# The feed-forward's output product with its 544 token columns cut as 512 and 32 instead of 272 and 272

## The reference

```python
def swiglu(x, w_in, w_out):
    gate, up = jnp.split(x @ w_in, 2, axis=-1)      # w_in (1024, 2*2816)
    return (jax.nn.silu(gate) * up) @ w_out         # w_out (2816, 1024)

for l in range(DEPTH):                              # DEPTH = 2
    x = layer_norm(DN_ALPHA * x + 0.5 * swiglu(x, ffn1_w_in[l], ffn1_w_out[l]), ...)
    ...                                             # projections, RWKV-7, attention, gated DeltaNet
    x = layer_norm(DN_ALPHA * x + mix, ...)
    x = layer_norm(DN_ALPHA * x + 0.5 * swiglu(x, ffn2_w_in[l], ffn2_w_out[l]), ...)
```

## Time and profile before

| what | value |
|---|---|
| runs | 2839.8, 2860.64 us; median 2850.22 |
| profiled execution, span | 2839.4 us; the faster run is 0.4 us longer |
| PE matmul busy | 2612.6 us (92%) |
| PE weight loads busy | 2457.6 us (87%) |
| VectorE (DVE) busy | 1667.0 us (59%) |
| ScalarE (ACT) busy | 946.3 us (33%) |
| POOL busy | 161.5 us (6%) |
| DMA | 201.67 MB, mean 71 GB/s |
| mean granted TensorE clock | 0.941 of full speed |

### The profile page before, as it was taken

How to read it: one execution, slowest core, us unless ns; L and a number is a source line. 1 busy time by engine, 2 the same in 40 slices (tenths; PEclk the granted TensorE clock), 3 DMA queues, 4 the chain that set the end, 5 groups by cost and what they waited for, 6 DMA issues and landing times.

```text
span 2839.4 us, 59246 instructions
## 1 busy us (share of the span) xinstructions
PE 2612.6 (92%) x23238; PEld 2457.6 (87%) x23238; DVE 1667.0 (59%) x2503; ACT 946.3 (33%) x1694; POOL 161.5 (6%) x168
## 2 busy tenths in 40 slices
PE   8999999978877899999999999998787789999996
PEld 8999999866665899999999999987666568999996
DVE  5666436665666466663366653477556655666534
ACT  4333224342222243332233332333322324333323
POOL 1030110000000010001100001100000001000011
PEclk9999999987887999999999999999877889999997
DMA  4853324310000323323222323341000022232221
GB/s 109 98 96 89 90 81 124 94 33 5 10 10 22 98 75 89 87 81 90 84 77 87 89 83 89 112 118 46 29 2 9 10 73 69 82 89 84 85 87 57
DMA packets 380501, 201.67 MB, mean 71 GB/s; under 512 B 41461, under 2 KB 376821, under 8 KB 379528
## 3 DMA queue, kind: packets, MB, share of 16 engines
q1 hardware_dynamic: 377928, 197.46, 24.1%
q0 software_dynamic: 2400, 1.82, 2.0%
HBM read 188.07 MB, written 13.34 MB: 71 GB/s over the span
## 4 chain that ended last, share of the span: by engine, by line
PE 76%; DVE 11%; issue 6%; ACT 5%; DMA 1%; SPq 1%; DVEq 0%; POOLq 0%; ACTq 0%; POOL 0%
PE ps L683 54%; PE ps L738 20%; DVE ar L1932 3%; DVE ar L1926 2%; ACT ar L1427 2%; ACT wh L1358 1%; DVE wl L1810 1%; SPq L530 1%; PE ps L1014 1%; DVE x L1926 1%; DMA raws<-in_ffn_w_in 0%; DVE ar L1962 0%; DVE xl L1917 0%; DVE ar L1929 0%; DMA raws<-in_w_in 0%
## 5 line engine op out<-in xcount | busy, mean ns | idle before, releaser
L1810 DVE TENSOR_TENSOR wl<-raws,wh 128x1024 fp32r<-128x1024 f32 x336 | 411.3, 1225 | 662.1 <-ACT wh L1358 658.0
L683 PE MATMUL ps<-xh,wh 128*128 128x272 f32 x2880 | 604.8, 291 | 17.7 <-DVE wl L1810 15.2
L683 PE MATMUL ps<-xh,wl 128*128 128x272 f32 x2880 | 599.7, 290 | 0.0
L683 PE MATMUL ps<-xl,wh 128*128 128x272 f32 x2880 | 598.2, 289 | 0.0
L738 PE MATMUL ps<-ar 64*64 64x64 f32 (+12 forms) x5408 | 423.5, 270 | 140.0 <-ACT ar L1427 37.1
L738 PEld LDWEIGHTS ps<-ar 64*64 64x64 f32 (+5 forms) x5408 | 317.2, 157 | 224.5 <-issue 58.8
L1358 ACT ACTIVATE wh<-raws 128x1024 fp32r<-128x1024 f32 x336 | 354.9, 1057 | 408.3 <-PE ps L683 375.9
L683 PEld LDWEIGHTS ps<-xh,wh 128*128 128x128 f32 x2880 | 457.5, 190 | 21.6 <-DVE wl L1810 17.9
L683 PEld LDWEIGHTS ps<-xl,wh 128*128 128x128 f32 x2880 | 457.7, 190 | 0.0
L683 PEld LDWEIGHTS ps<-xh,wl 128*128 128x128 f32 x2880 | 457.2, 190 | 0.0
L683 PE MATMUL ps<-hh,wh 128*128 128x272 f32 x1408 | 292.2, 289 | 0.0
(11 more groups left out here) (190 smaller groups left out, 2678.4 us busy)
## 6 DMA issues: line engine op xcount, KB each, us to landing
raws<-in_ffn_w_in SPq DMA_DIRECT2D x176, 512.0 KB, 3.6
raws<-in_ffn_w_out SPq DMA_DIRECT2D x64, 512.0 KB, 4.0
raws<-in_w_in SPq DMA_DIRECT2D x42, 512.0 KB, 3.7
raws<-in_ffn_w_out SPq DMA_DIRECT2D x32, 384.0 KB, 3.4
raws<-in_w_out SPq DMA_DIRECT2D x16, 448.0 KB, 3.9
x_kept<-x SPq DMA_DIRECT2D x2, 2176.0 KB, 10.2
x<-x_kept SPq DMA_DIRECT2D x2, 2176.0 KB, 8.0
ar<-in_consts SPq DMA_DIRECT2D x2, 1337.5 KB, 6.7
```

The costliest lines, as they stand in the source:

```text
L683: ins = pe.matmul(ps[:, bank + h, 0:n1 - h * NH], w[u % 2][:, k, :], a[:, k0 + k, h * NH:n1], start=(first and k == 0 and n == 0), stop=(l ...
L1810: dve.tensor_tensor(wl[u % 2][:, :, :], raw[u % 2][:, :, :], wh[u % 2][:, :, :].bitcast(F32), ALU.subtract).then_inc(sem("wl_done"), 1)
```

## The change

The matmul helper cuts the columns at 512 (`SEQ`) instead of at 272 (`NH`) where the activations are `hh`, that is in the output product alone. The first matmul of each pair fills one bank with 512 columns, the second puts the last 32 into the next bank. The residual reads the 544 results as one contiguous run over both banks (`tokens`) instead of as two runs of 272 (`bank2`). Everything else stays.

```diff
+        def tokens(b):
+            return ps[:, b:b + 2, :].rearrange("p a n -> p (a n)")[:, 0:NT]
...
                     for n, (w, a) in enumerate(((wh, hi), (wh, lo), (wl, hi))):
+                        cut = SEQ if hi is hh else NH
                         for h in range(2):
-                            n1 = a.shape[2] if h else NH
-                            ins = pe.matmul(ps[:, bank + h, 0:n1 - h * NH], w[u % 2][:, k, :], a[:, k0 + k, h * NH:n1],
+                            n1 = a.shape[2] if h else cut
+                            ins = pe.matmul(ps[:, bank + h, 0:n1 - h * cut], w[u % 2][:, k, :], a[:, k0 + k, h * cut:n1],
                                             start=(first and k == 0 and n == 0), stop=(last and k == nblocks - 1 and n == 2))
...
-                dve.scalar_tensor_tensor(out=halves(chunk(x, c + u)), in0=halves(chunk(x, c + u)), scalar=ALPHA, in1=bank2(2 * u),
+                dve.scalar_tensor_tensor(out=chunk(x, c + u), in0=chunk(x, c + u), scalar=ALPHA, in1=tokens(2 * u),
                                          op0=ALU.mult, op1=ALU.add).then_inc(sem("z_done"), 1)
```

## The result

The changed kernel takes 3039.27 us in the median of two runs (3034.34 and 3044.19), against 2850.22 before: a ratio of 1.067, 95% interval 1.063 to 1.071. The profiled execution took 3044.19 us with a span of 3042.0 us, 202.6 over the span before.

What follows compares the result with a forecast made beforehand. TensorE's matmuls were taken to bound the kernel. A pair at 225 + 112 = 337 ns against 250.5, 86.5 ns more over 2112 pairs, gave +183 us and 3026 us, range 2985 to 3110.

Steps and rivals of the forecast that it cites:

- first part: Whole kernel: TensorE busy 92% of 2839.4 us and never waiting in the output product, so pair time is paid in full.
- parts 2 and 3: Output product's pairs: the 512 hides the 32's load, 225 ns; the 32 cannot hide the next load, 112 ns.
- part 3: Output product's 32-column matmul: paced by the weight load for the next 512, 112 ns, ends 108 and 125.
- part 2: Output product's 512-column matmul: 225 ns, the 12.0 ns over the stream taken as per instruction; ends 213 and 236.
- the cold stretch: Stretch at clock 0.5: 272-column matmuls 225 ns each against 226.7 of stream, taken to show the excess is not in columns.
- parts 5 and 6: VectorE's residual, costed at nothing; ScalarE, VectorE, POOL, SP keep their instructions, weight splits and DMAs get more room.
- rival B: Output product: the granted clock falls to the lower level, 643 ns a pair, +829 us, 3669 us; chance 3%.
- Rival A: Output product: weight loads reach two deep and stay hidden, 227 to 251 ns a pair, -50 to 0 us; chance 7%.
- rival C: Output product: 32-column matmuls cost more than their load, at quarter rate and not overlapped, +295 us, 3135 us; chance 7%.

Runs made afterwards that it cites:

- the run in phases: Changed kernel with all 24 (or 18) 512-column matmuls of each granule first, then all 32-column ones; ratio 1.0903 to the kernel before.

## Why the prediction held

- *PE is the bound, and a pair's price is paid in full* (first part): held. 193 us of the 203 lie in the four stages.
- *The load is hidden behind one stream and no deeper; the 32 can't cover it* (parts 2 and 3): shown by the three cuts, by halving the load (-53 ns) and by widening the second matmul (+16 ns for 240 columns). One sign was described wrongly: the starts aren't 225 and 112 ns apart in turn but about 25 and 315, as the 512 is recorded as started while its load still runs. The load of the 512 does start with the 32, as forecast.
- *The slot at 112 ns* (part 3): it is 107 by subtraction, near the lower end, 108, which had been read from the exposed load; the cuts at 384 and 320 give 109 and 111. 112 is right for narrow matmuls behind one another, as the run in phases repeats.
- *The 512 at 225 ns* (part 2): mis-sized. It is 235, next to the upper end, 236. The argument that the cold stretch shows no excess per column was wrong: it only shows that there is none at 1.2 GHz. That the excess disappears at half the clock fits a limit in time per column, and I read it as a cost per instruction. The two errors, 10 ns too little and 5 too much, cancel by half, which is luck: 337 against 341.7, +183 against +193 us.
- *Residual, ScalarE, VectorE, DMA cost nothing* (parts 5 and 6): held; 712 to 723 ns again, and the cut at 288 with the contiguous read is level with before.
- *The clock* (rival B): 1.00 in all four stages. The price that was given for it is real, though, when the narrow matmuls stand in runs of 24.
- *Rival A* (loads two deep) and *rival C* (narrow matmuls at a quarter of the rate): refuted by the pair itself and by the cut at 320 and 224. The sustained 131 ns for 512 columns with a load, which the Trainium skill gives (page "TensorE: Matmul & The Clock Gate", "Back-to-back issue gap"), isn't what this trace has: 234 to 235 ns, and the measurement decides.
- The time: 3026 forecast, 3039 measured. Some 10 us of that are the pair's 4.7 ns more.

## What to carry to other kernels

When two matmuls share the work of one weight block, give both at least as much stream as a load takes; what counts is the narrower one, and filling the bank to 512 columns buys nothing if it leaves a remainder behind. Read the price of an uncovered load from the first matmul after a wait, and check whether an excess over the stream is per instruction or per column before scaling it: two widths decide it, one does not. And if narrow matmuls are needed, mix them with wide ones rather than collecting them.

## What the runs showed of the hardware that was not expected

- fp32r columns stream at 0.45 to 0.46 ns each at the granted clock of 1.00 (125.3 ns for 272, 234 to 235 for 512), 10% over the 0.417 of 2.4 GHz; at clock 0.50 there is no such excess (225 ns for 272, rounded, where 1.2 GHz gives 226.7). At clock 0.50 a 512 takes 0.43 us, again without excess. bf16 operands lower it, packed ones by 10.6 ns a pair more than strided ones: packed, a 512 has about 215 ns. Why fp32r has the excess is not shown.
- A load of fp32r weights costs 0.83 ns a column when exposed: 107 ns for 128, 54 for 64. A load of 128 columns of bf16 weights costs 27 ns at most, so 512 and 32 columns in bf16 hardly pay for the second matmul: 240.7 ns a pair against 226.7 of stream.
- Runs of 24 narrow matmuls, 2.7 us with no idle time, were followed by a granted clock of 0.50 for 3.4 us, nine times in the first output product; runs of three never were.
